# Dividing the 64 chunks of the expert up stage anew: 16 / 32 / 16 in place of 12 / 48 / 4

## The reference

```python
q = (xc @ w_q)                      # 8 heads x 2 halves x 128
s1, s2 = q1 @ k1.T, q2 @ k2.T       # 128 sub-keys each
v1, i1 = top_k(s1, 16); v2, i2 = top_k(s2, 16)
top_s, top_pos = top_k(v1[:, None] + v2[None, :], 16)
ids = i1 * 128 + i2 at top_pos      # 16384 experts
g = softmax(top_s)
y = sum over heads and top 16 of g * gelu(u[ids] . x) * v[ids]
```

## Time and profile before

| | us |
|---|---|
| median of 3 runs | 3676.2 (3674.93 to 3680.64) |
| profiled execution, its own time | 3681.08 |
| its span in the trace | 3678.9 |
| PE / DVE / ACT / POOL busy | 96% / 74% / 39% / 25% |

### The profile page before, as it was taken

The page is one execution under the profiler, slowest core; times in us unless marked ns, Lnnn a source line. Parts: engine busy times, 40 slices in busy tenths (PEclk is TensorE's granted clock), DMA queues, the critical chain, the costliest instruction groups (busy, mean ns, idle before and its releaser), DMA issues.

```text
span 3678.9 us, 56602 instructions
## 1 busy us (share of the span) xinstructions
PE 3549.7 (96%) x19806; PEld 3172.4 (86%) x19806; DVE 2712.5 (74%) x5637; ACT 1423.4 (39%) x1857; POOL 919.3 (25%) x593
## 2 busy tenths in 40 slices
PE   7999999989999999999999999998899998999998
PEld 7888788989999977778788887888899998888787
DVE  5665439988888678888766644399878885788887
ACT  5554333334444333333355533333344443333333
POOL 1000013532222244444200000135222221444441
PEclk9999999999999999999999999999999999999999
DMA  3112322568888899999721133224788889999995
GB/s 140 46 46 103 137 98 81 171 247 289 294 306 293 313 344 367 365 379 369 268 81 46 46 126 137 86 100 154 263 303 300 292 292 329 337 375 363 371 377 223
DMA packets 217380, 851.54 MB, mean 231 GB/s; under 512 B 19504, under 2 KB 69056, under 8 KB 168496
## 3 DMA queue, kind: packets, MB, share of 16 engines
q1 hardware_dynamic: 120944, 478.99, 35.7%
q0 software_dynamic: 74432, 270.53, 20.6%
q10 hardware_dynamic: 21888, 100.67, 6.6%
HBM read 747.36 MB, written 102.76 MB: 231 GB/s over the span
## 4 chain that ended last, share of the span: by engine, by line
PE 72%; DVE 16%; DMA 5%; issue 3%; ACT 3%; SPq 0%; ACTq 0%; DVEq 0%
PE bank L1284 20%; PE bank L1039 15%; PE bank L1041 14%; PE bank L1040 14%; PE bank L1261 5%; DMA raw<-in_stream 4%; DVE rows L918 2%; DVE lo L665 2%; PE bank L1148 1%; DVE rows L923 1%; DVE h L956 1%; DMA gate_in<-gate_d 1%; PE bank L1125 1%; DVE top_i L876 1%; DVE left L870 1%
## 5 line engine op out<-in xcount | busy, mean ns | idle before, releaser
L665 DVE TENSOR_TENSOR lo<-raw,hi 128x2048 fp32r<-128x2048 f32 x316 | 723.9, 2291 | 420.8 <-ACT hi L414 420.1
L1039 PE MATMUL bank<-xT_hi,hi 128*128 128x384 f32 (+1 forms) x2688 | 961.3, 358 | 5.0 <-DVE lo L665 2.4
L1041 PE MATMUL bank<-xT_hi,lo 128*128 128x384 f32 (+1 forms) x2688 | 940.6, 350 | 0.0
L1040 PE MATMUL bank<-xT_lo,hi 128*128 128x384 f32 (+1 forms) x2688 | 938.2, 349 | 0.0
L414 ACT ACTIVATE hi<-raw 128x2048 fp32r<-128x2048 f32 x356 | 682.5, 1917 | 373.2 <-PE bank L1284 219.3
L1039 PEld LDWEIGHTS bank<-xT_hi,hi 128*128 128x128 f32 x2688 | 509.3, 189 | 35.7 <-issue 8.2
L403 POOL DMA_INDIRECT rows<-in_u_rows,ids x256 | 296.1, 1156 | 938.3 <-DVE act_row L953 837.2
L1040 PEld LDWEIGHTS bank<-xT_lo,hi 128*128 128x128 f32 x2688 | 509.0, 189 | 24.3
L1041 PEld LDWEIGHTS bank<-xT_hi,lo 128*128 128x128 f32 x2688 | 507.5, 189 | 26.0
L403 POOL DMA_INDIRECT rows<-in_v_rows,ids x256 | 407.8, 1593 | 460.8 <-DVE h L956 385.2
L1284 PE MATMUL bank<-hi,w_hi 128*128 128x512 f32 x1536 | 487.6, 399 | 20.8 <-DVE w_lo L994 20.8
(11 more groups left out here) (195 smaller groups left out, 4824.5 us busy)
## 6 DMA issues: line engine op xcount, KB each, us to landing
raw<-in_stream SPq DMA_DIRECT2D x356, 1024.0 KB, 5.2
act_d<-act_s ACTq DMA_DIRECT2D x128, 384.0 KB, 5.3
gate_d<-gate_s ACTq DMA_DIRECT2D x24, 2048.0 KB, 9.5
act_in<-act_d SPq DMA_DIRECT2D x128, 384.0 KB, 7.2
gate_in<-gate_d SPq DMA_DIRECT2D x32, 1536.0 KB, 13.6
rows<-in_u_rows,ids POOLq DMA_INDIRECT x256, 6.1
rows<-in_v_rows,ids POOLq DMA_INDIRECT x256, 9.2
h<-in_x SPq DMA_DIRECT2D x1, 2048.0 KB, 9.4
```

The source lines that it names most:

```text
L665: dve.tensor_tensor(lo[s][:], raw[s][:], hi[s][:].bitcast(F32), ALU.subtract).then_inc(lo_done, 1)
L1039: pe.matmul(dst, a_[0], b_[0], start=first, stop=False)
L1040: pe.matmul(dst, a_[0], b_[1], start=False, stop=False)
L1041: return pe.matmul(dst, a_[1], b_[0], start=False, stop=last)
```

## The change

The 64 chunks of the up stage become 16 while the search ends, 32 with three groups of gate products each (one after the first half, two after the second), and 16 without. The transposes come after chunks 12 to 14 (before 9 to 11), the exponential at chunk 8 (before 7). GpSimd keeps its splits up to chunk 12, waits for `ids`, issues the first 8 fetches, splits chunks 13 to 16, and goes on with the fetches. VectorE does the first 8 row ops ahead of the gate part, then 2 per chunk with gates and 3 per chunk of the tail: 120 of the 256 in the up stage (before 104), and the other 136 over 62 chunks of the down stage (before 152 over 61).

```diff
-FIND_STEPS = 12
-EXP_STEP, IDX_STEP = 7, 9
+FIND_STEPS = 16
+EXP_STEP, IDX_STEP = 8, 12
-G_RING, G_PER_STEP, G_TOK = 4, 2, 4
+G_RING, G_PER_STEP, G_TOK = 4, 3, 4
-U_ROWS_PER_STEP, V_ROWS_PER_PAIR = 2, 5
-U_ROW_OPS = U_ROWS_PER_STEP * (C_U - FIND_STEPS)
+EARLY_ROWS, G_ROWS, TAIL_ROWS = 8, 2, 3
+ROWS_STEP = 12
+U_ROW_OPS = EARLY_ROWS + G_ROWS * G_STEPS + TAIL_ROWS * (C_U - FIND_STEPS - G_STEPS)
+V_ROW_OPS = ROW_OPS - U_ROW_OPS
+V_ROW_CHUNKS = C_V - 2
-FIRST_PAIR, REST_PAIR = 0, 7
+FIRST_PAIR, REST_PAIR = 0, 5
...
                 split_lo(lp + P_WQ, 1)
-                with pool.Fori(1, C_WQ // 2 + J_G) as j:
+                with pool.Fori(1, C_WQ // 2 + ROWS_STEP // 2) as j:
                     for s in range(2):
                         split_lo(lp + P_WQ + j, s)
-                split_lo(lp + P_U + J_G, 0)
+                split_lo(lp + P_U + ROWS_STEP // 2, 0)
...
                 wait_alone(pool, ids_done, l + 1, pool_passed)
-                for n in range(ROW_OPS):
...
+                fetch_rows(0, NR)
+                for c in range(ROWS_STEP + 1, FIND_STEPS + 1):
+                    split_lo(lp + P_U + c // 2, c % 2)
+                fetch_rows(NR, ROW_OPS)
...
+                for n in range(EARLY_ROWS):
+                    row_op(n)
                 dve.wait_ge(lo_done, 2 * (lp + P_U + J_G) + 1 + CR)
                 wait_alone(dve, idx_ev, NDT * (l + 1) + 1, dve_passed)
...
-                    for n in range(U_ROWS_PER_STEP):
-                        row_op(st * U_ROWS_PER_STEP + n)
+                    for _ in range(G_ROWS if st < G_STEPS else TAIL_ROWS):
+                        row_op(n)
+                        n += 1
...
-                with pe.Fori(0, G_STEPS // 2) as it:
-                    for s in range(2):
+                with pe.Fori(0, G_STEPS // G_RING) as it:
+                    for st in range(G_RING):
                         for i in range(2):
-                            experts(J_G + it, s, i)
-                            gates_of(l * GROUPS + it * 4 + s * 2 + i, s * 2 + i)
+                            experts(J_G + it * (G_RING // 2) + st // 2, st % 2, i)
+                            for q in range(st * G_PER_STEP + i, st * G_PER_STEP + 2 * i + 1):
+                                gates_of(l * GROUPS + it * (G_RING * G_PER_STEP) + q, q % G_RING)
```

More of the change, by code:

```diff
@@ L83 @@
 SLICES = TD // SLICE
-SLICE_STEPS = SLICE // (G_TOK * G_PER_STEP)
+PER_SLICE = SLICE // G_TOK
 V_LOADS, I_PER_LOAD = 16, 8
@@ L392, in _, with fetch_rows @@
                 split_lo(lp + P_WQ, 1)
-                with pool.Fori(1, C_WQ // 2 + J_G) as j:
+                with pool.Fori(1, C_WQ // 2 + ROWS_STEP // 2) as j:
                     for s in range(2):
                         split_lo(lp + P_WQ + j, s)
-                split_lo(lp + P_U + J_G, 0)
-                wait_alone(pool, ids_done, l + 1, pool_passed)
-                for n in range(ROW_OPS):
[L401 to L405, removed]
+                split_lo(lp + P_U + ROWS_STEP // 2, 0)
+                def fetch_rows(first, end):
+                    for n in range(first, end):
+                        if n >= NR:
+                            wait_alone(pool, row_done, ROW_OPS * l + n - NR + 1, pool_passed)
+                        pool.indirect_dma_start(rows[:, n % NR], None, a["u_rows" if n < P else "v_rows"],
+                                                bass.IndirectOffsetOnAxis(ids[:, n % P:n % P + 1], 0)
+                                                ).then_inc(rows_in[n % NR], 16)
+                wait_alone(pool, ids_done, l + 1, pool_passed)
+                fetch_rows(0, NR)
+                for c in range(ROWS_STEP + 1, FIND_STEPS + 1):
+                    split_lo(lp + P_U + c // 2, c % 2)
+                fetch_rows(NR, ROW_OPS)
         @block.scalar
@@ L589, in _ @@
                     tt = st - IDX_STEP
-                    if tt >= 0:
+                    if 0 <= tt < NDT:
                         act.wait_ge(idx_ps, l * NDT + tt + 2)
@@ L595, in _, with g_evac @@
                     store_act(st // 2, st % 2)
[L597 to L601, removed]
+                def g_evac(q):
+                    w, sl = q // PER_SLICE // 2, q // PER_SLICE % 2
+                    act.wait_ge(g_ps, l * GROUPS + q + 1 + G_RING)
+                    if q % PER_SLICE == 0 and not w == l == 0:
@@ L602, in g_evac @@
                         act.wait_ge(gate_out[sl], 16 * (l * SLICES // 2 + w))
                     src = ps[4 + q % G_RING][:].rearrange("p (t i) -> p i t", t=G_TOK)
-                    dst = gate_s[:, sl, :, q * G_TOK:(q + 1) * G_TOK]
+                    dst = gate_s[:, sl, :, q % PER_SLICE * G_TOK:(q % PER_SLICE + 1) * G_TOK]
                     act.activation(dst, src, ACT.Copy).then_inc(g_ev, 1)
[L607 to L616, removed]
-                            store_act(j, s)
-                        act.wait_ge(g_ev, l * GROUPS + (w * 2 + sl + 1) * SLICE // G_TOK + G_RING)
-                        act.dma_start(gate_d[w * 2 + sl], gate_s[:, sl].rearrange("p i t -> p (i t)")).then_inc(gate_out[sl], 16)
@@ L621, in _, with store_gates @@
-                g_slices(0)
-                with act.Fori(1, SLICES // 2) as w:
-                    g_slices(w)
+                def store_gates(w):
+                    act.wait_ge(g_ev, l * GROUPS + (w + 1) * PER_SLICE + G_RING)
+                    act.dma_start(gate_d[w], gate_s[:, w % 2].rearrange("p i t -> p (i t)")).then_inc(gate_out[w % 2], 16)
+                for st in range(G_STEPS):
+                    j, s = J_G + st // 2, st % 2
+                    ahead(lp + P_U + j, s)
+                    for b in range(G_PER_STEP):
+                        q = st * G_PER_STEP + b
+                        if b < 2:
+                            gelu(j, s, b)
+                        g_evac(q)
+                        if b == 1:
+                            store_act(j, s)
+                        if q % PER_SLICE == PER_SLICE - 1:
+                            store_gates(q // PER_SLICE)
@@ L964, in weigh_rows @@
                     dve.wait_ge(row_weighed, 2 * l + part + 1)
+                for n in range(EARLY_ROWS):
+                    row_op(n)
                 dve.wait_ge(lo_done, 2 * (lp + P_U + J_G) + 1 + CR)
                 wait_alone(dve, idx_ev, NDT * (l + 1) + 1, dve_passed)
+                n = EARLY_ROWS
                 for st in range(C_U - FIND_STEPS):
@@ L996, in _ @@
                 weigh_step(0)
-                n = U_ROW_OPS
+                assert n == U_ROW_OPS
                 for c in range(C_V - 1):
@@ L1004, in _ @@
                         weigh_rows(1, FIRST_ROWS, P)
-                    while n < min(ROW_OPS, U_ROW_OPS + (c + 1) * V_ROWS_PER_PAIR // 2):
+                    while n < U_ROW_OPS + min(c + 1, V_ROW_CHUNKS) * V_ROW_OPS // V_ROW_CHUNKS:
                         row_op(n)
```

## The result

The changed kernel takes 3700.7 us (median of 6 runs, 3699.5 to 3702.7), the kernel before 3677.1 on the same occasions: a ratio of 1.0064, 95% interval 1.0051 to 1.0077. It is 23.6 us slower, and the interval of the ratio is 19 to 28 us; forecast were 21.4. The profiled execution has a span of 3700.8 us, 21.9 more than before.

The account below looks back on a forecast made before the run. TensorE, 96% busy, was taken as the bound. Per layer 9.7 (later up stage) + 2 (gate load) - 1 (down stage) = 10.7, so 21.4 on 3681.1 gives 3702.5, less 4.9 for the median about 3698 us; range 3683 to 3715.

Parts of the forecast that it names:

- The end of the up stage before: In the kernel before, TensorE's remaining chunks, groups and a restart put the end of the up stage at 1284.6.
- The split of chunk 13 behind `ids` and eight fetches: End of search: GpSimd's late split leaves TensorE idle 38 us, chunk 13 starting at 782.0 (bounds 778.9 and 784.5).
- `ids` stays where it is: End of search: with the same number of splits ahead, `ids` keeps its 763.07, only 0.3 earlier.
- The rival in which it moves forward by 10 us: Search: splits hold look-ups less, `ids` comes earlier, to 752.7 or before; with 17.0 gained, 3664; 4 in 100 for faster.
- The restart: After a TensorE stop the clock stays at its lower level, 1.2 GHz, for a while, costing 2.56 us.
- The lock between VectorE and GpSimd: Row products fall on the last four of eight fetches; the eight take 12.9 us, 10.4 undisturbed.
- The part with gates: 32 chunks with three groups take 10.97 us each, 351.0 in all, TensorE still setting the pace.
- VectorE was no bound: Rival for the gate part: VectorE's step passes 10.97; at 11.5 it costs 17 per layer, 3732; 6 in 100.
- The tail: 16 chunks without gates at 8.32 us, 133.1 in all; up stage ends at 1294.3, 9.7 later than before.
- Its rival, that transfers hold it: Tail: transfers set the pace; half the bound costs 4 per layer, 3706, all of it 3715; 12 in 100.
- The gate load: Before the down stage: two more fetches share the lines with it, costing 0 to 2.8 us per layer, 2 taken.
- The down stage: Fewer row ops per chunk, 2.2 from 2.5, give back at most 1.4 us per layer; 1 taken.

Follow-up runs that it names:

- first: Changed kernel with GpSimd splitting all chunks up to 16 ahead of its wait for the expert numbers: 3663.9 us, ratio to the kernel before 0.9966.
- second experiment: Changed kernel with all splits up to chunk 16 ahead of the wait and no early row products: 3631.9 us, ratio to the kernel before 0.9883.
- fifth: Changed kernel with four fetches and four early row products in place of eight: 3689.2 us, ratio to the kernel before 1.0027.
- fourth experiment: Changed kernel with two rows per chunk of the tail instead of three: 3695.7 us, ratio to the kernel before 1.0058.

## Why the prediction was right, point by point

- **The end of the up stage before** was reckoned at 1284.6; the last of its matmuls starts at 1284.28, so 1284.5.
- **The split of chunk 13 behind `ids` and eight fetches**: right in mechanism, shown by the stop that vanishes when the splits come first (first and second experiment) and that shrinks with the number of fetches (fifth). Size: chunk 13 at 780.65 against 782.0; the eight fetches took 12.1 against 12.9 and the split 4.8 against 5.2.
- **`ids` stays where it is**: 762.48 against 763.07, 0.6 earlier. The rival in which it moves forward by 10 us was never near. The second experiment shows the opposite sign: four more splits move it back by 9 us.
- **The restart** was reckoned at 2.56 us over the 8.32 of a chunk: chunk 13 takes 10.83 (780.65 to 791.48), and the granted clock is 0.51 from 781 to 786, its lower level.
- **The lock between VectorE and GpSimd** cost the fetches less than I priced: the three that met row products grew by 0.4 to 0.9 us each. What I had not seen is the other direction. Once the splits ran, it was the row products that waited, and this cost TensorE nothing. VectorE's timeline after:

```profile
774.94 1.23 DVE L961 CUSTOM_DVE_ANT_0 rows<-rows,x_row 128x1024 f32<-128x1024 f32 x1
...
776.63 4.97 DVE L961 CUSTOM_DVE_ANT_0 rows<-rows,x_row 128x1024 f32<-128x1024 f32 x1 [0.46 <-DMA rows<-in_u_rows,ids]
...
781.53 5.57 DVE L961 CUSTOM_DVE_ANT_0 rows<-rows,x_row 128x1024 f32<-128x1024 f32 x1
```

  A row product of 1.23 us takes 4.97 and 5.57 beside two splits. The Trainium skill ("SBUF — State Buffer", section "SBUF: two separate sides") says that the second comer waits for the whole of the first. The trace agrees: the split of chunk 13 ends at 780.52, and the row product that began beside it ends at 781.60, 1.08 later.
- **The part with gates** is the term that was mis-sized: I took 0.11 us off each chunk for two groups back to back. No row showed such a pair. The chain has the pairs of groups at these places:

```profile
1149.79 1.78 PE bank L1273 x16
1160.85 1.78 PE bank L1273 x16
```

  11.06 us per chunk against the 10.97 of the sum, 2.7 us per layer more. The pair saves 0.02, not 0.11. VectorE was no bound: TensorE 340.00 of 340 us, VectorE 309, 91% against the 92% reckoned.
- **The tail** at 8.32 per chunk with three rows: TensorE 125.00 of 125 at 367 GB/s. Its rival, that transfers hold it, did not come. The end of the up stage is 1295.6 against 1294.3.
- **The gate load** was priced at 2 per layer and cost 2.0 and 2.7. Its cause is the third fetch (fourth experiment). The size came out right by luck: taking the third fetch away wins 3.5 to 5.6 us, not 2. The loads of the kernel before, with two rows as well, landed later (18.26 and 19.16) than those of the fourth experiment (14.66 and 18.47); why, no run shows.
- **The down stage** gave back 1.5 in the first layer (544.6 to 543.2 from the start of the first product to that of the last) and 2.7 in the second (544.8 to 542.2), against 1 reckoned.

This makes 11.2 + 2.0 - 1.5 = 11.7 us for the first layer and 10.1 + 2.7 - 2.7 = 10.2 (before rounding) for the second, where 10.7 each was said. The path, the releaser and the direction were right for the reasons given. That the sum fits within 1 us, 21.9 against 21.4, is partly luck: chunk 13 came 1.4 us earlier than said and the part with gates took 2.7 longer, and what the gate load cost beyond its price in the second layer, the down stage gave back.

## What to carry to other kernels

When work of one engine is spread over a longer stage, look for everything that feeds it in that stage and at where each feeder's queue waits for something else: here four more chunks of TensorE's work were put under the search, but the split that feeds the second of them stayed behind the result of that search, on a third engine. Operands of the bound engine go ahead of the wait, side work behind it. And a load that ends a stop is moved in the size that the stop needs: on the changed kernel 1.5 MB early won 20 us and 3 MB early won nothing. The stream load behind 3 MB landed some 17 us late and that behind 1.5 MB some 8.5, and in both cases all but about 7 to 8 us of it reached TensorE.

## What the runs showed that I had not expected

- A GpSimd split beside look-ups with two SBUF inputs slows both: 5.85 to 6.20 against 4.62 us for the split, 4.38 against 2.29 for the look-up.
- A one-input operation of VectorE between them, the shift of the index table (L940), took 2.19 to 2.20 us in the first two experiments, where it takes 0.23 when no split runs.
- The stream load behind two gate loads held ScalarE for 13.4 us and TensorE for 10, while one gate load in the same place delayed TensorE by 0.7 to 1.3 us.
